# Key, value and query projections in one-pass products, with the queries projected inside the attention loop

## The reference

```python
def kv_rows(x, g_kv, w_kv):
    h = rms_norm(x, g_kv)
    kv = (h @ w_kv).reshape(x.shape[0], x.shape[1], N_BRANCH, 2, KV_HEADS, HEAD_DIM)
    return kv[:, :, 0], kv[:, :, 1], kv[:, :, 2]

def nsa_query_side(x, g_pre, w_in):
    u = rms_norm(x, g_pre) @ w_in
    q = u[..., :Q_WIDTH]                              # 1024 columns
    z = u[..., Q_WIDTH:Q_WIDTH * (1 + N_BRANCH)]      # 3 x 1024 columns
    gate = sigmoid(u[..., Q_WIDTH * (1 + N_BRANCH):]) # 48 columns

# in nsa_block, per branch: scores, bias, masked softmax, values
lw = jnp.einsum('btkgd,bskd->bkgts', q, kw).astype(f32) * scale + bias_w
```

## Time and profile before

| | us |
|---|---|
| runs | 991.15, 1070.59, 993.01 |
| median | 993.01 |
| the profiled execution | 990.91 |
| its span on the core | 989.1 |
| PE busy | 920.6 (93%) |
| granted clock of PE, mean | 0.992 |
| VectorE / ScalarE / GpSimd busy | 503.2 / 421.7 / 301.0 |

### The profile page before, as it was taken

How to read it: one execution, slowest core, us unless ns; L and a number is a source line. 1 busy time by engine, 2 the same in 40 slices (tenths; PEclk the granted TensorE clock), 3 DMA queues, 4 the chain that set the end, 5 groups by cost and what they waited for, 6 DMA issues and landing times. The chain is left out here.

```text
span 989.1 us, 16539 instructions
## 1 busy us (share of the span) xinstructions
PE 920.6 (93%) x6238; PEld 774.8 (78%) x6238; DVE 503.2 (51%) x1131; ACT 421.7 (43%) x872; POOL 301.0 (30%) x311
## 2 busy tenths in 40 slices
PE   2799999998999999998998899999999999799995
PEld 2699999944479878887998878878988888587663
DVE  2477999965843450212011255555555564635663
ACT  4356677523412411311223256555656555513321
POOL 0269888771460000003000033343332432500000
PEclk9999999999999999999999899999999999999998
DMA  8345443157446051135543222222222100932621
GB/s 213 85 107 170 118 111 77 49 167 256 153 121 215 38 173 53 33 96 127 135 85 85 45 43 65 44 65 66 43 55 52 46 2 2 243 132 66 179 91 32
DMA packets 156069, 97.40 MB, mean 98 GB/s; under 512 B 97156, under 2 KB 144932, under 8 KB 155911
## 3 DMA queue, kind: packets, MB, share of 16 engines
q1 hardware_dynamic: 141134, 77.07, 29.3%
q0 software_dynamic: 4896, 10.32, 3.1%
q10 hardware_dynamic: 9961, 8.97, 2.8%
HBM read 87.48 MB, written 18.85 MB: 108 GB/s over the span
## 5 line engine op out<-in xcount | busy, mean ns | idle before, releaser
L725 ACT ACTIVATE arena<-psum 128x256 f32<-128x256 f32 (+10 forms) x221 | 89.2, 441 | 217.5 <-PE psum L1623 58.6
L1623 PE MATMUL psum<-arena 128*128 128x256 f32 (+2 forms) x832 | 170.5, 367 | 1.2 <-issue 1.2
L1623 PEld LDWEIGHTS psum<-arena 128*128 128x128 f32 (+1 forms) x832 | 146.5, 190 | 22.6 <-issue 2.3
L1244 DVE SCALAR_TENSOR_TENSOR psum<-arena,psum 128x512 f32<-128x512 f32 x168 | 127.0, 756 | 6.0
L704 POOL TENSOR_SCALAR arena<-arena,kept 128x512 f32<-128x512 f32 (+3 forms) x128 | 82.7, 661 | 141.5 <-DVE kept L1490 141.5
L1943 PE MATMUL psum<-u_hi,tile_hi 128*128 128x288 f32 x352 | 113.1, 321 | 8.4 <-ACT arena L725 7.7
L1642 PE MATMUL psum<-h_hi,tile_hi 128*128 128x288 f32 x384 | 115.2, 300 | 4.1 <-DVE tile_lo L1216 4.1
L1643 PE MATMUL psum<-h_lo,tile_hi 128*128 128x288 f32 x384 | 114.6, 299 | 0.0
L1644 PE MATMUL psum<-h_hi,tile_lo 128*128 128x288 f32 x384 | 114.2, 297 | 0.0
L1944 PE MATMUL psum<-u_lo,tile_hi 128*128 128x288 f32 x352 | 104.3, 296 | 0.0
L1945 PE MATMUL psum<-u_hi,tile_lo 128*128 128x288 f32 x352 | 103.8, 295 | 0.0
(11 more groups left out here) (256 smaller groups left out, 1655.8 us busy)
## 6 DMA issues: line engine op xcount, KB each, us to landing
tile_whole<-in_b_w_in SPq DMA_DIRECT2D x64, 256.0 KB
tile_whole<-in_a_w_in SPq DMA_DIRECT2D x24, 512.0 KB
arena<-in_cmp_w SPq DMA_DIRECT2D x3, 2048.0 KB, 9.7
arena<-in_w_kv SPq DMA_DIRECT2D x6, 1024.0 KB, 12.2
bias_copies<-bias_line POOLq DMA_DIRECT2D x4, 1280.0 KB, 24.1
arena<-in_x_prompt SPq DMA_DIRECT2D x8, 512.0 KB, 10.2
arena<-in_a_w_out SPq DMA_DIRECT2D x4, 1024.0 KB, 16.8
arena<-bias_copies SPq DMA_DIRECT2D x16, 256.0 KB, 3.7
```

The lines of the kernel that those rows point to most:

```text
L725: return nc.scalar.activation(out, in_, ACT.Copy, scale=scale)
L1244: V.scalar_tensor_tensor(out=acc_p, in0=glu_p[:, m, w:w + SEQ], scalar=tap, in1=acc_p, op0=ALU.mult, op1=ALU.add).then_inc(S["conv_step"], 1)
L1623: ins = pe.matmul(out, l, r, start=(k == 0), stop=(k == len(pairs) - 1))
```

## The change

Keys and values: the transposed rows `kvh` and the six weight chunks `kvw` are split into `hi` (ScalarE, `kv_rows_hi`, `kv_weight_hi`) and `lo` (VectorE, `kv_rows_lo`, `kv_weight_lo`). Of thirty jobs become fifteen: one for each branch and row tile, with k and v beside each other as 512 moving columns, in three one-pass products (`three`). Queries: only tile 0 is made ahead of the loop, beside the gate and two z tiles. The other seven stand in one `stream` with the z tiles, which the loop works off in bank 7, four tiles in five steps. A finished query half is read by ScalarE (`q_hi`) and then by VectorE (`q_lo`, and the samples' queries). The transposed keys and the compressed keys are split once (`kt_hi`, `kt_lo`, `kcbd_hi`, `kcbd_lo`), and all scores of the prompt are three one-pass products, with the two heads of a pair in turn. The splits of the first weight tiles stand behind the key/value products, since these weights now fill their slots of the ring.

```diff
@@ -308,9 +331,12 @@
         C_KV = len(chunks)
         chunks += [cols(I["w_kv"], c * CH) for c in range(6)]
         C_Q = len(chunks)
-        chunks += [tile_cols(b_w, 0, m) for m in range(KD)]
-        C_Z = len(chunks)
-        chunks += [tile_cols(b_w, D * (1 + br), m) for m in range(KD) for br in range(NBR)]
+        stream = [("q", 0), ("z", 0), ("z", 1)]
+        for m in range(KD - 1):
+            stream += [("z", NBR * m + 2), ("q", m + 1), ("z", NBR * m + 3), ("z", NBR * m + 4)]
+        stream.append(("z", NBR * KD - 1))
+        N_TILES, AHEAD = len(stream), 3
+        chunks += [tile_cols(b_w, 0, n) if kind == "q" else tile_cols(b_w, D * (1 + n % NBR), n // NBR) for kind, n in stream]
...
@@ -324,12 +350,44 @@
         def kv_at(c, t):
-            return 10 * (c // 2) + (4 * (c % 2) + t if t < 4 else 8 + c % 2)
...
+        PARTS = (((0, 0, 0, 8), (0, 1, 0, 4)), ((0, 1, 4, 8), (1, 0, 0, 8)), ((2, 0, 0, 8), (1, 1, 0, 8)),
+                 ((2, 1, 0, 8), (3, 0, 0, 4)), ((3, 0, 4, 8), (3, 1, 0, 8)))
+
+        def tile_parts(n):
+
+            if n >= 5 * KD:
+                return (None, None)
+            first = AHEAD + 4 * (n // 5)
+            return [(first + i, hf, range(lo, hi)) if first + i < N_TILES else None for i, hf, lo, hi in PARTS[n % 5]]
...
+            def kv_rows_hi(t):
+                act.wait_ge(S["hu_ready"], 2 * (t + 1))
+                act.wait_ge(S["o_mm"], t + 1)
+                here = slice(t * P, t * P + rows(t))
+                copy(kvh_hi[:, :, here], kvh_whole[:, :, here]).then_inc(S["hh_ready"], 1)
+
+            def kv_weight_hi(c):
+                act.wait_ge(place[C_KV + c][2], arrived[C_KV + c])
+                if c >= 4:
+                    act.wait_ge(S["kv_mm"], 5)
+                copy(kvw_hi(c // 2)[:, c % 2], kvw_whole[:, (4, 5, 0, 1, 2, 3)[c]]).then_inc(S["hi_ready"], 1)
...
+                if t >= 2:
+                    kv_rows_hi(t - 2)
+                if t in (2, 3):
+                    kv_weight_hi(t - 2)
+            kv_rows_hi(TT - 2)
+            kv_rows_hi(TT - 1)
...
+            for n in range(3 * TT):
+                br, t = n // TT, n % TT
+                if n == 1:
...
+                if n in (1, 2):
+                    kv_weight_hi(n + 1)
+                if n in (6, 7):
+                    kv_weight_hi(n - 2)
...
-                if n == 24:
-                    split_hi(0)
-                    split_hi(1)
...
+            act.wait_ge(S["kv_mm"], 3 * TT)
+            for j in range(3):
+                split_hi(j)
...
             compress_p_silu(0, 1)
...
+            split_hi(3)
+            act.wait_ge(S["tile_mm"], 1)
+            copy(q_hi[:, 0, 0:HT], pb(0, HT), QSCALE).then_inc(S["qk_hi"], 1)
+            copy(q_hi[:, 0, HT:SEQ], pb(1, SEQ - HT), QSCALE).then_inc(S["qk_hi"], 1)
+            copy(q_first, pb(1, HT)[:, SEQ - HT:HT], QSCALE).then_inc(S["qk_hi"], 1)
+            split_hi(4)
+            act.wait_ge(S["kt_ready"], 2 * TT)
+            for br in range(2):
+                copy(kt_hi[:, br], kt[:, br]).then_inc(S["qk_hi"], 1)
             act.wait_ge(S["gate_mm"], 1)
...
+            def kv_rows_lo(t):
+                dve.wait_ge(S["hh_ready"], TT + t + 1)
+                here = slice(t * P, t * P + rows(t))
+                V.tensor_tensor(out=kvh_lo[:, :, here], in0=kvh_whole[:, :, here], in1=kvh_hi[:, :, here], op=ALU.subtract).then_inc(S["hl_ready"], 1)
+
+            def kv_weight_lo(c):
+                dve.wait_ge(S["hi_ready"], C_OA + c + 1)
+                V.tensor_tensor(out=kvw_lo(c // 2)[:, c % 2], in0=kvw_whole[:, (4, 5, 0, 1, 2, 3)[c]], in1=kvw_hi(c // 2)[:, c % 2],
+                                op=ALU.subtract).then_inc(S["lo_ready"], 1)
...
+                    if t >= 3:
+                        kv_rows_lo(t - 3)
+                    if t in (3, 4):
+                        kv_weight_lo(t - 3)
+            for t in range(2, TT):
+                kv_rows_lo(t)
+            for c in range(2, 6):
+                kv_weight_lo(c)
...
+            split_lo(2)
+            split_lo(3)
+
+            def q_rest(out, src, hi):
+                V.scalar_tensor_tensor(out=out, in0=src, scalar=QSCALE, in1=hi, op0=ALU.mult, op1=ALU.subtract).then_inc(S["qk_lo"], 1)
+
+            dve.wait_ge(S["qk_hi"], 3)
+            q_rest(q_lo[:, 0, 0:HT], pb(0, HT), q_hi[:, 0, 0:HT])
+            q_rest(q_lo[:, 0, HT:SEQ], pb(1, SEQ - HT), q_hi[:, 0, HT:SEQ])
+            split_lo(4)
+            dve.wait_ge(S["qk_hi"], 5)
+            for br in range(2):
+                V.tensor_tensor(out=kt_lo[:, br], in0=kt[:, br], in1=kt_hi[:, br], op=ALU.subtract).then_inc(S["qk_lo"], 1)
...
+            def q_drain(part):
+
+                if not part or part[2][-1] < KD - 1 or stream[part[0]][0] == "z":
+                    return
+                m, hf = stream[part[0]][1], part[1]
+                dve.wait_ge(S["qk_hi"], 6 + 2 * (m - 1) + hf + 1)
+                here = slice(hf * HT, min(hf * HT + HT, SEQ))
+                q_rest(q_lo[:, m % 2, here], pb(7, here.stop - here.start), q_hi[:, m % 2, here])
+                if hf:
+                    q_samples(m, pb(7, HT)[:, SEQ - HT:HT], QSCALE)
...
-            for n in range(30):
-                c, t = kv_jobs[n]
-                await_chunk(C_KV + c)
+            def three(out, w, x, first, last):
+                pe.matmul(out, w[0], x[0], start=first, stop=False)
+                pe.matmul(out, w[0], x[1], start=False, stop=False)
+                return pe.matmul(out, w[1], x[0], start=False, stop=last)
+
+            for n in range(3 * TT):
+                br, t = n // TT, n % TT
+                pe.wait_ge(S["lo_ready"], 1 + 2 * br + 2)
                 if n == 2:
                     turn_b(TT - 1)
                 if n < 2:
-                    pe.wait_ge(S["hu_ready"], 2 * (n + 1))
                     pe.wait_ge(S["o_scaled"], 4)
                 elif n < 6:
-                    pe.wait_ge(S["hu_ready"], 2 * TT if n >= 4 else 2 * (n + 1))
                     pe.wait_ge(S["o_scaled"], TT)
+                    pe.wait_ge(S["hu_ready"], 2 * TT if n >= 4 else 8)
                 else:
-                    pe.wait_ge(S["kv_ready"], n - 5)
-                if t < 4:
-                    if c < 2:
-                        lhs = hT[:, :, (t // 2) * 256 + t % 2:(t // 2) * 256 + 256:2]
-                    else:
-                        lhs = hT[:, :, t * P:(t + 1) * P]
-                    product(pb(kv_bank(n), CH), ((lhs[:, k], chunk_sb(C_KV + c)[:, k]) for k in range(KD))).then_inc(S["kv_mm"], 1)
-                elif c % 2:
-
-                    for k in range(KD):
...
+                    pe.wait_ge(S["kv_ready"], 2 * (n - 5))
+                if n < 5:
+                    pe.wait_ge(S["hl_ready"], TT + (2, 2, 4, 4, 5)[n])
+                r = rows(t)
+                tokens = slice((t // 2) * 256 + t % 2, (t // 2) * 256 + 256, 2) if br == 0 and t < 4 else slice(t * P, t * P + r)
+                for k in range(KD):
...
-            for m in range(KD):
...
-                tile_product(2 * (m % 3), m).then_inc(S["q_mm"], 1)
...
+            tile_product(0, 0).then_inc(S["tile_mm"], 1)
+            pe.wait_ge(S["lo_ready"], 6 + 3)
             split_product(6, wgate_hi, wgate_lo).then_inc(S["gate_mm"], 1)
-            pe.wait_ge(S["q_ready"], 7)
+            pe.wait_ge(S["bd_ready"], 4)
+            tile_product(2, 2).then_inc(S["tile_mm"], 1)
+            pe.wait_ge(S["qk_hi"], 3)
+            pe.wait_ge(S["qk_lo"], 2)
+            tile_product(0, 3).then_inc(S["tile_mm"], 1)
...
-                    if u >= 4:
-                        pe.wait_ge(S["l_ready"], u - 3)
-                    if br == 0:
-                        for ir in range(4):
-                            ins = pe.matmul(pb(u % 4, 4, 64)[:, ir], qT[:, m, (3 - ir) * P:(4 - ir) * P], kcbd[:, m // 4],
-                                            start=True, stop=True)
-                    else:
-                        i, half = qs[k // 2], k % 2
-                        head = slice(HD * half, HD * half + HD)
-                        ins = pe.matmul(pb(u % 4, P * (i + 1)), qT[head, m, i * P:(i + 1) * P], kt[head, br - 1, m // 4, 0:P * (i + 1)],
-                                        start=True, stop=True)
+                if br == 0:
+                    pe.wait_ge(S["qk_lo"], q_low(m, 1) if m else 5)
+                    if us[0] >= 4:
+                        pe.wait_ge(S["l_ready"], us[0] - 3)
+                    for ir in range(4):
+                        here, out = slice((3 - ir) * P, (4 - ir) * P), pb(us[0] % 4, 4, 64)[:, ir]
+                        pe.matmul(out, q_hi[:, m % 2, here], kcbd_hi[:, m // 4], start=True, stop=False)
+                        pe.matmul(out, q_hi[:, m % 2, here], kcbd_lo[:, m // 4], start=False, stop=False)
+                        ins = pe.matmul(out, q_lo[:, m % 2, here], kcbd_hi[:, m // 4], start=False, stop=True)
```

(13 more changed lines are left out.)

280 lines of the change are left out of this document (141 added, 139 removed).

## The result

| | before | changed |
|---|---|---|
| median, us | 992.52 (4 runs) | 1003.57 (4 runs) |
| lowest to highest | 991.15 to 1070.59 | 1002.29 to 1006.56 |
| ratio, 95% interval | | 1.011 [1.0083, 1.0136] |
| span of the profiled execution | 989.1 | 1000.7 |
| granted clock of PE, mean | 0.992 | 0.974 |

What follows compares the result with a forecast made beforehand. TensorE, busy 93% and working in fixed order, was taken as the bound, so waits before its full stages add up. Terms summed to +9.7 us, span 998.8, forecast 1001 us (range 984 to 1024), called "same" within 2%.

Steps and rivals of the forecast that it cites:

- Term 1: Key/value products: 360 one-pass matmuls of 512 columns at 0.2257 us replace 94.0 us of four-pass ones, −12.7 us.
- 2 first wait: Key/value stage start: first job waits for VectorE's low halves behind row tile 4's norm, +10.7 us.
- 3 second wait: Before the third key/value job: PE waits for VectorE's multiplies and low halves after tile 4's transposes, +3.9 us.
- Term 4: Key/value stage: PE runs at reduced clock after the two waits, the second perhaps partly spared, +4.4 us.
- Term 5: Behind the key/value products: K copies wait for ScalarE's and VectorE's splits, moving everything behind by +4.3 us.
- Term 6: Compressed product to first scores: wait or slow clock falls from 8.7 to 7.6 us, −1.1 us.
- 7, 8 loop: Loop: seven query tiles move in at no net cost, 0, and scores change by +0.2 us.
- Term 8: Loop scores: head products −4.8, compressed scores +4, waits on bank 7 +1; together +0.2 us.
- Rival A: Loop head products: fp32r products of two head halves don't run side by side, +10 to +21 us; chance 0.20.
- Rival B: Key/value lead-in: waits and slow clocks at lower ends or hidden, total 971 to 978 us; chance 0.08.
- Rival C: Loop: draining bank 7 through two engines stops PE about 1 us per query half, total 1015; chance 0.07.

Runs made afterwards that it cites:

- e2: On top of e1, VectorE makes the low halves of row tiles 2 and 3 ahead of tile 4's gains: 987.89 us, ratio 0.9947.
- e1: Changed kernel, VectorE makes low halves of row tile 1 and second weight chunk before the norm of row tile 4: 993.34 us, ratio 1.0005.
- e6: Changed kernel with 88 overwritten one-pass matmuls on PE in the wait ahead of the key/value products: 1001.5 us, ratio 1.0104.
- e3: Changed kernel, VectorE's splits of first query tile and gate weights moved behind its K and compression-row copies: 998.83 us, ratio 1.0059.
- e5: Edits of e1, e2 and e3 together, plus PE's second z tile moved behind K's second-half compression and its compressed product: 974.19 us, ratio 0.9828.
- e7: Changed kernel, each head's three one-pass products placed together instead of the two heads in turn: 1008.72 us, ratio 1.0159.
- e9: Changed kernel with unsplit float32 key/value products in the same 15 jobs, sample rows' k and v paired on PE's column halves: 995.85 us, ratio 1.0055.

## Why the prediction was right

Forecast 1001 and no change beyond 2%, measured 1003.57; the sum on the span was +9.7, measured +11.6.

| term | forecast | measured | from |
|---|---|---|---|
| 1 products | −12.7 | −10.7 | 360 × 0.2315 = 83.3 against 94.0 |
| 2 first wait | +10.7 | +10.4 | transposes to first product, 0.93 before, 11.30 now |
| 3 second wait | +3.9 | +3.7 | row of 387.75; e2 |
| 4 clock | +4.4 | +4.3 | 13 products slow after the first wait, 2.6 (e1: 2.5, e6: 2.6); about 9 after the second, 1.7 |
| 5 behind the products | +4.3 | +5.8 | ledger, 5.49 + 0.28; e3 |
| 6 before the loop | −1.1 | −4.1 | ledger, −48.55 + 44.5 |
| 7, 8 loop | +0.2 | +3.1 | ledger, (9.13 + 37.12 − 44.5) + 1.33, with the query tiles taken off once |

(Term 6 and the loop share the 44.5 us of query tiles; −4.1 takes them out of the first, and the loop's 46.25 + 1.33 less 44.5 is +3.1.) The measured column adds up to +12.5. The transposes of row tile 3 started 0.6 us earlier in the changed kernel's trace (358.21 against 358.84; 357.67 to 359.35 in the other runs), and 0.3 is what the key/value stage holds beside its products, waits and clock: +11.6.

**Terms 1 to 4** had the mechanism right. Term 1 was too large by 2 us: 512 one-pass columns take 0.2315 from start to start, where the fixed surplus gave 0.2257 and the proportional one 0.2354. The surplus over 2.4 GHz does grow with the columns, from 12 ns at 288 to 18 at 512. The Trainium skill ("TensorE: Matmul & The Clock Gate", Back-to-back issue gap) has a formula for an isolated product on a warm engine, from which I estimate 215.8 ns at 512 columns, and about 131 ns in a stream; the trace shows 231.5 and agrees with neither. (131 ns would have made term 1 −46.8, not −46.) The part of the argument that weighed most, the order of VectorE around tile 4's norm, was confirmed by e1 and e2: without a change in work, 16.2 us by ratio are gone. Term 4 allowed that the second wait might be partly spared, and it was: the slow clock came three products late and cost 1.7, against 2.6 behind the first.

**Term 5** was too small by 1.5. The wait itself was forecast to the tenth: 4.68 instead of 0.39, +4.3. (ScalarE's three parts there add up to 2.8, not 2.9.) But I took PE's clock after it as free. The eight transposes that follow took 1.97 for 1.10 and the next eight 1.99 for 1.54 with the gap between their halves; shorter waits for VectorE's copies gave back a part, and from the end of the wait to the compression it is 7.5 us for 6.3. e3 took it all back (5.55 in this piece of its trace). The rule that I used in term 4, a wait and then some 2 us at half clock, should have been applied to each of the new waits.

**Term 6** had the right sum with the clock at the wrong place. It put 2.3 us of slow clock ahead of the loop, from the two z tiles in the earlier trace rows. With the z tiles moved ahead of the compression, PE's last wait (3.75) stands directly before the first scores, and these and the first tile pieces run slow: the first m is 9.13 − 6.36 = +2.8 longer. −4.1 and +2.8 are together −1.3, against −1.1. e5 shows the link: with work in front of the scores, 4.3 us of it went.

**Term 8.** The head products take 36.07 us in all 32 steps, 40.92 before: −4.85, forecast −4.8. The step is 1.18 with 512 and 128 columns and 1.07 with 384 and 256. The twelve small products of a compressed-score step take 1.435 against 0.93 between their neighbours: +0.5 in each of seven m, as forecast; the first m's took 2.55, since it ran at the slow clock. The chain of waits in the changed kernel has one step of each:

```profile
578.88 1.18 PE psum L2072 x11
...
588.12 1.07 PE psum L2072 x10
```

Rival A is out: fp32r products on half of PE's rows do run in pairs. Rival B is out with the first product at 369.5. Rival C is out as well. PE's waits at the drain of bank 7 in the loop are 8.4 us in 8 places, 7.7 in 8 before, and none is for VectorE:

```profile
PE psum L2042 <- ACT arena L757: 8.4, 8, 1.2
```

(The last number of such a row, in the earlier trace rows too, is the longest wait and not the mean.)

**Left over** is +1.33, and it lies in the last m: 36.9 us for 35.5, with 125.9 behind it in both traces. PE is busy for 30.7 of the 36.9 (29.75 of the 35.5 before), so it waits for others there; 0.5 is the longer compressed scores. What the rest is was not tested, and term 8 had this m a little shorter.

That the total came within 2 us on the span is in part luck. Term 1 saved 2.0 less than forecast and term 5 cost 1.5 more; terms 2 to 4 together cost 0.6 less, and the 0.9 of start and stage remainder, which no term had, went the same way. Term 6 (−3.0) and the loop (+2.9) cancel, since the slow clock moved from one to the other.

## What to carry to other kernels

When an engine runs out of a long queue in fixed order, an operand that must be prepared is priced by where its preparation stands in the other engines' orders, not by how long it takes: 3.5 us of subtracts behind one late norm cost 10.4, and the same subtracts in front of it cost nothing. Count each new wait of TensorE as its length and the slow clock behind it, 1.5 to 2.8 us here for waits of 3.7 us and more. A change that measures as a small loss may hold a gain and a few misplaced waits: here reordering alone turned 1.011 into 0.983.

## What the runs showed of the hardware

- Two one-pass products on the two halves of PE's rows start within 25 ns of each other and take the time of one (0.23 us at 512 columns), even when three of one head stand before those of the other (e7).
- After waits of 10.2, 3.7, 4.7 and 3.75 us the granted clock was at the 1.2 GHz level for 5.6, 3.7, some 11 and 6.6 us (0.427 for 512 columns against 0.2315). Behind the 3.7 us wait it fell only after three products. e6 removed it behind the first wait by keeping PE at work.
- The slow clock can come without a long wait: before the change the first products of the compression, behind transposes with gaps of 0.2 to 1.2 us, were 0.214 apart up to 468.2 and 0.112 from there. In e5 nearly all of them ran at 0.112 and the compression took 8.43 instead of 10.05.
- A float32 product of 64 rows and 512 columns took as long as one with 128 rows (6.9 us for eight); only side by side on two halves of the columns did it get cheaper (3.67 for both, e9).
- A small one-pass product, 64 columns, is 0.10 to 0.12 us from the next, little less than one of 288 columns (0.132).
